# Depthwise convolution of 31 taps: TensorE's share goes from 14 taps on 64-wide diagonals to 16 taps on 32-wide diagonals, and the work around it moves between engines

## Chip, cores and metric

The kernel runs as one program on 1 core of a Trainium2 chip. The metric is the time of one execution in device microseconds (us); the median of several executions is given, and one further execution was profiled. A core has TensorE (PE, with its weight loads shown as PEld), VectorE (DVE), ScalarE (ACT), GpSimd (POOL) and SyncE (SP), each with its own instruction queue.

## What is computed

The reference is a two-layer mixed model over 512 tokens of width 1024 (an mLSTM layer, an attention layer, then a second block with its own two layers), all in float32. The change lies in one place, the convolution module of the second block's second layer:

```python
def conformer_conv(h, w_pw1, b_pw1, w_dw, b_dw, ln_g, ln_b, w_pw2, b_pw2):
    a, gate = jnp.split(h @ w_pw1 + b_pw1, 2, axis=-1)
    y = a * jax.nn.sigmoid(gate)
    y = lax.conv_general_dilated(y, w_dw[:, None, :], window_strides=(1,),
                                 padding=[(CONV_K // 2, CONV_K // 2)],
                                 dimension_numbers=('NWC', 'WIO', 'NWC'),
                                 feature_group_count=CONV_W) + b_dw
    y = jax.nn.silu(layernorm(y, ln_g, ln_b))
    return y @ w_pw2 + b_pw2
```

With `CONV_K = 31` and `CONV_W = 1024`, each channel is convolved along the 512 tokens with its own 31 taps.

## The kernel before

Activations lie with channels on the 128 partitions: a tile is 128 channels by 512 tokens, and a width of 1024 is 8 tiles. Every large product is done as three float32r products (hi by hi, lo by hi, hi by lo), so ScalarE makes a rounded copy of each weight chunk (`split_hi`, L509) and VectorE the remainder (`split_lo`, L514). A chunk is 128x1024; four slots are in flight, and SyncE loads the next chunk when VectorE has made the low part of the one before it in the slot.

The stage `p_1` computes `h @ w_pw1` in 8 groups. Group g gives one tile of `a` and one of `gate` in two PSUM banks of `G`: 48 matmuls of 128x128 by 512 (L2378), two chunks. Each engine goes through the groups in program order, and they meet through semaphores:

- ScalarE per group: two `split_hi` for the chunks of group g+2 (each waits until TensorE has used the chunk in that slot), then in `glu` the sigmoid of `gate` (L2094), and when VectorE has written `yp`, two copies of 64 partitions each into `yp_turned` (L2099), which holds the tile with its halves exchanged.
- VectorE per group: two `split_lo`, then in `glu` the product `yp` = (a + bias) * sigmoid (L2185), stored with 15 columns of zeros at both ends, and 17 taps of the convolution as shifted multiply-adds on `yp`, alternating between the accumulators `Y[g]` and `S[2]` (L2192, L2194 for taps 0 and 1, L2198 for taps 2 to 16). Then `total_low` (L2174) adds one PSUM bank of the group before, L2202 adds the two accumulators, `total_high` (L2180) adds the other bank.
- TensorE per group: the 48 matmuls, and behind them `taps(g-1)`, the other 14 taps of the group before: each tap is a product with a diagonal matrix, kept as 64x64 blocks in `tap_diag`. Seven taps read `yp` (L2015) and seven read `yp_turned` (L2018), so that the four 64x64 quarters of the array work on different data. Each of these float32 matmuls shows as two passes in the trace. Group g uses the banks 2p and 2p+1 of `M` (p = g mod 2), so `taps(g)` needs only that the totals of group g-2 are done (`cv_d >= g + 1`; two of the counts are there from the start).
- GpSimd makes the diagonals of a group in two operations of 128x448 (L2344, L2347) once the taps of two groups before are done.

After the last group VectorE adds the banks of group 7, TensorE sums the channels (L2027: 8 matmuls with `ones`, each waiting for its tile), VectorE subtracts the mean (L2212), ScalarE squares (L444), TensorE sums the squares (L2447), ten filling matmuls follow (`keep_warm`, L348), and then the stage `p_2`.

```python
                pe.wait_ge(cv_w, 2 * g + 2)
                wait_read(pe, "p_1", g)
                pe.wait_ge(cv_x, 2 * g + 4)
                pe.wait_ge(cv_d, g + 1)
```

## Time and profile before

| | |
|---|---|
| median of 3 runs | 2579.09 us (2578.74 to 2581.74) |
| the profiled execution, its own time | 2582.74 us |
| its span in the profile | 2580.9 us |
| PE busy | 2515.6 us, 97% of the span |
| DVE busy | 1544.0 us, 60% |
| ACT busy | 1028.7 us, 40% |
| POOL busy | 98.1 us, 4% |
| DMA | 266.86 MB, mean 103 GB/s |

The profile is of one execution. Its span runs from the first to the last instruction; the execution's own time is 1.8 us longer. Shares are averages over the whole program, in which the stage `p_1` takes some 150 us (from 2005 to about 2152 us), so what bounds that stage is read from its stretch of the trace. In timelines the first column is the start in us from the span's start, the second the duration, then engine, line, operation, output and inputs.

### The profile page before, as it was taken

How to read it: one execution, taken by the hardware profiler on the slowest of the kernel's cores; microseconds unless marked ns; L12 is line 12 of the kernel's file. 1: busy time of each engine (PE TensorE's matmuls, PEld its weight loads, DVE VectorE, ACT ScalarE, POOL GpSimd, SP SyncE). 2: the span in 40 equal slices, each digit the busy share in tenths (PEclk: the TensorE clock that was granted, in tenths of full speed). 3: DMA queues.
4: the chain of work that ended last, by engine and by line, in shares of the span. 5: the costliest groups of instructions: out<-in, count | busy, mean ns of one | idle time of the engine just before them, and what ended most of it. 6: DMA issues, size and time to landing. Idle time of an engine off the chain costs nothing.

```text
span 2580.9 us, 31514 instructions
## 1 busy us (share of the span) xinstructions
PE 2515.6 (97%) x12534; PEld 2005.1 (78%) x12534; DVE 1544.0 (60%) x2581; ACT 1028.7 (40%) x1583; POOL 98.1 (4%) x133
## 2 busy tenths in 40 slices
PE   7999999999999989999999998999999999999999
PEld 6887788888886667888878876888887665888887
DVE  6455775877455656746576256666654997533433
ACT  4444543434435555434345345423323324422323
POOL 0000001010000000000000000011100110000000
PEclk9999999999999999999999999999999999999999
DMA  5422335554221122332324221366642121233331
GB/s 155 134 83 90 92 96 171 154 175 137 67 82 58 55 69 76 96 98 83 100 88 153 82 66 42 124 195 194 189 146 90 58 66 45 86 98 98 98 95 52
DMA packets 285080, 266.86 MB, mean 103 GB/s; under 512 B 13331, under 2 KB 270663, under 8 KB 284935
## 3 DMA queue, kind: packets, MB, share of 16 engines
q1 hardware_dynamic: 268503, 210.33, 26.5%
q0 software_dynamic: 15024, 54.33, 7.1%
q8 instruction: 99, 1.62, 0.3%
q14 instruction: 46, 0.38, 0.0%
q10 hardware_dynamic: 1408, 0.20, 0.0%
HBM read 262.72 MB, written 2.10 MB: 103 GB/s over the span
## 4 chain that ended last, share of the span: by engine, by line
PE 87%; DVE 8%; ACT 2%; issue 2%; SPq 1%; DMA 0%; POOL 0%; ACTq 0%; DVEq 0%; POOLq 0%
PE G L2378 71%; PE G L2394 7%; DVE Y L2198 2%; DVE S L2198 1%; DVE w_lo L514 1%; PE M L2447 1%; PE M L818 1%; PE M L1196 1%; PE M L828 1%; PE M L1185 1%; PE M L1207 1%; PE M L1659 1%; PE M L1670 1%; PE M L2428 1%; DVE S L612 0%
## 5 line engine op out<-in xcount | busy, mean ns | idle before, releaser
L514 DVE TENSOR_TENSOR w_lo<-raw,w_hi 128x1024 fp32r<-128x1024 f32 x396 | 484.2, 1228 | 647.6 <-ACT w_hi L509 646.6
L2378 PE MATMUL G<-H_hi,w_hi 128*128 128x512 f32 (+1 forms) x2016 | 801.4, 398 | 4.9 <-DVE H_lo L377 1.6
L2378 PE MATMUL G<-H_hi,w_lo 128*128 128x512 f32 (+1 forms) x2016 | 783.9, 389 | 0.0
L2378 PE MATMUL G<-H_lo,w_hi 128*128 128x512 f32 (+1 forms) x2016 | 783.4, 389 | 0.0
L509 ACT ACTIVATE w_hi<-raw 128x1024 fp32r<-128x1024 f32 x396 | 416.9, 1056 | 890.2 <-PE G L2378 794.6
L2378 PEld LDWEIGHTS G<-H_hi,w_hi 128*128 128x128 f32 x2016 | 380.0, 188 | 108.9 <-issue 28.9
L2378 PEld LDWEIGHTS G<-H_hi,w_lo 128*128 128x128 f32 x2016 | 379.5, 188 | 79.3
L2378 PEld LDWEIGHTS G<-H_lo,w_hi 128*128 128x128 f32 x2016 | 379.9, 188 | 77.8 <-issue 3.8
L2378 PE MATMUL G<-hid_hi,w_hi 128*128 128x512 f32 x864 | 337.9, 391 | 5.3 <-DVE hid_lo L633 3.9
L2378 PE MATMUL G<-hid_lo,w_hi 128*128 128x512 f32 x864 | 336.9, 390 | 0.0
L2378 PE MATMUL G<-hid_hi,w_lo 128*128 128x512 f32 x864 | 336.7, 390 | 0.0
L2378 PEld LDWEIGHTS G<-hid_hi,w_hi 128*128 128x128 f32 x864 | 162.5, 188 | 42.0 <-DVE hid_lo L633 5.6
L2378 PEld LDWEIGHTS G<-hid_hi,w_lo 128*128 128x128 f32 x864 | 162.6, 188 | 33.9
L2378 PEld LDWEIGHTS G<-hid_lo,w_hi 128*128 128x128 f32 x864 | 162.6, 188 | 33.4
L2394 PE MATMUL G<-w_hi,H_hi 128*128 128x256 f32 x480 | 140.4, 292 | 3.5 <-DVE w_lo L514 2.1
L612 DVE SCALAR_TENSOR_TENSOR S<-SQ,VT,S 128x511 f32<-128x511 f32 (+1 forms) x176 | 128.2, 750 | 19.6 <-ACT S L574 16.5
L2394 PE MATMUL G<-w_hi,H_lo 128*128 128x256 f32 x480 | 136.5, 284 | 0.0
L2394 PE MATMUL G<-w_lo,H_hi 128*128 128x256 f32 x480 | 136.4, 284 | 0.0
L694 DVE SCALAR_TENSOR_TENSOR mod_acc<-mod_w,cs,mod_acc 128x512 f32<-128x512 f32 x168 | 125.9, 750 | 3.4
L672 POOL DMA_DIRECT2D mod_w<-in_w_mod x96 | 69.7, 726 | 1039.1 <-DVE mod_acc L694 470.6
L2394 PEld LDWEIGHTS G<-w_hi,H_hi 128*128 128x128 f32 x480 | 92.6, 193 | 14.9 <-issue 8.3
L574 ACT ACTIVATE S<-SQ,VT 128x512 f32<-128x512 f32 x88 | 67.0, 809 | 88.4 <-DVE SQ L619 88.4
(352 smaller groups left out, 2422.7 us busy)
## 6 DMA issues: line engine op xcount, KB each, us to landing
raw<-in_w_ff SPq DMA_DIRECT2D x128, 512.0 KB
mod_w<-in_w_mod POOLq DMA_DIRECT2D x96, 512.0 KB, 4.5
raw<-in_ffn_w_up SPq DMA_DIRECT2D x176, 256.0 KB
raw<-in_ffn_w_down SPq DMA_DIRECT2D x32, 512.0 KB
raw<-in_w_in SPq DMA_DIRECT2D x28, 512.0 KB
raw<-in_mlstm_w_in SPq DMA_DIRECT2D x24, 512.0 KB
raw<-in_kv_w SPq DMA_DIRECT2D x16, 512.0 KB
raw<-in_fox_w_qg SPq DMA_DIRECT2D x16, 512.0 KB
```

The costliest lines, as they stand in the source:

```text
L509: act.activation(w_hi[:, j, :], raw[:, j, :], ACT.Copy).then_inc(hi_done, 1)
L514: dve.tensor_tensor(w_lo[:, j, :], raw[:, j, :], w_hi[:, j, :], ALU.subtract).then_inc(lo_done, 1)
L574: act.activation(S[:, h, :], SQ[:, h, :], ACT.Identity, bias=VT[:, ds(t + cb, 1)], scale=VT[:, ds(t + (cw + 88), 1)]).then_inc(f_a, 1)
L612: return dve.scalar_tensor_tensor(S[:, h, k:T], SQ[:, h, 0:T - k], w, S[:, h, k:T], ALU.mult, ALU.add)
L672: pool.dma_start(mod_w[:, n % 2], src[:, 2 * quarter:2 * quarter + 2, block * 512:block * 512 + 512]).then_inc(mod_landed[n % 2], 16)
L694: one = dve.scalar_tensor_tensor(acc[:, cols], w, c, acc[:, cols], ALU.mult, ALU.add)
L818: return pe.matmul(M[:, bank, col:col + T - s * P], mK[hs, h // 2, s * P:s * P + P], mQ[hs, h // 2, s * P:T], start=(col == 0), stop=True, ...
L828: mm = pe.matmul(M[:, 2 + b // 2, (b % 2) * (P + 1):(b % 2 + 1) * (P + 1)], m_part(h, s)[:, (b - s) * P:(b - s) * P + P], mV[:, s, h, :], ...
L1185: mm = pe.matmul(fox_scores(n, e)[:, 0:(b + 1) * P], xQ[hs, q, b * P:b * P + P], xK[hs, q, 0:(b + 1) * P], start=True, stop=True)
L2198: link.post(dve.scalar_tensor_tensor(acc, yp[:, p:p + 1, j:j + T], tap(j), acc, ALU.mult, ALU.add))
L2378: mm = pe.matmul(G[:, 2 * p + m, 0:n], lw[:, k, ms], rh[:, t, 0:n], start=(t == 0 and q == 0), stop=(t == st["ktiles"] - 1 and q == 2), sk ...
L2394: mm = pe.matmul(G[:, 2 * p + b // 2, (b % 2) * GC:(b % 2) * GC + GC], lh[:, t, bs], rw[:, k, :], start=(t == 0 and q == 0 and b % 2 == 0) ...
```

## The change

TensorE gets 16 taps (15 to 30), and VectorE and ScalarE keep 15.

- A diagonal is now held as 32x32 blocks. `yp` and three turned copies `yp_turned[0..2]` (turned by 32, 64 and 96 partitions) feed four taps each. For each tap four matmuls of 32x32 by 512 run, one for each quarter r of the rows, writing quarter r+d of bank r. So all four banks of `M` hold one group, and the sum of the four is the 16 taps. `taps(g)` therefore waits for the totals of group g-1 (`cv_d >= g + 2`).
- ScalarE makes the first tap with the bias (`Y[g]`, new line L2115), starts four DMAs for the copies turned by 32 and 96, makes the copy turned by 64 itself as before, and makes the 16 diagonals of 128x32 of a group, ahead of that group's two `split_hi`. GpSimd's operations in this stage are gone.
- VectorE has 14 taps (1 to 14); `total` adds four banks instead of two.
- Six of the eight channel sums stand ahead of the last group's taps on TensorE.
- ScalarE makes the 32-wide identity and the turned tap columns (16 small operations) once, ahead of the stage `s0_up0`. VectorE's zero fill covers the edges of the four padded tiles only.

```diff
-PE_TAPS = 14
-HALF_TAPS = PE_TAPS // 2
+COPIES, COPY_TAPS = 4, 4
+PE_TAPS = COPIES * COPY_TAPS
 V_TAPS = CONV_K - PE_TAPS
+QP = P // COPIES
...
+            def channel_sum(t):
+                pe.wait_ge(cv_d, t + 3)
+                return pe.matmul(G[:, 0, :], ones[:], Y[:, t, :], start=(t == 0), stop=(t == 7), skip_group_check=True)
+
             def taps(g, p):
                 if g == 1:
                     pe.wait_ge(mod_ok, 4)
-                pe.wait_ge(cv_w, 2 * g + 2)
+                if g == DT - 1:
+                    wait_read(pe, "p_1", DT - 2)
+                    for t in range(DT - 2):
+                        channel_sum(t)
+                pe.wait_ge(cv_w, g + 1)
                 wait_read(pe, "p_1", g)
-                pe.wait_ge(cv_x, 2 * g + 4)
-                pe.wait_ge(cv_d, g + 1)
-                low, high = slice(0, HP), slice(HP, P)
-                for j in range(HALF_TAPS):
...
+                pe.wait_ge(cv_x, 2 * g + 2)
+                pe.wait_ge(cv_r[p], 64 * (g // 2 + 1))
+                pe.wait_ge(cv_d, g + 2)
+                for j in range(COPY_TAPS):
+                    for d in range(COPIES):
+                        source = yp_turned[d - 1] if d else yp
+                        tap = V_TAPS + COPY_TAPS * d + j
+                        for r in range(COPIES):
+                            rs, cs = quarter(r), quarter(r + d)
+                            mm = pe.matmul(M[cs, r, :], tap_diag[rs, p, COPY_TAPS * d + j, :], source[rs, p, tap:tap + T],
+                                           start=(j == 0), stop=(j == COPY_TAPS - 1), skip_group_check=True)
                 mm.then_inc(cv_pe, 1)
 
             linear("p_1", H_hi, H_lo, need=from_h("odd"), behind=taps)
...
+            channel_sum(DT - 2)
+            channel_sum(DT - 1).then_inc(cv_s, 1)
...
             held(act, "n_out", split_hi)
+            for r in range(COPIES):
+                act.activation(quarter_ident[quarter(r), :], ident[quarter(r), quarter(r)], ACT.Copy).then_inc(cv_h, 1)
+                for d in range(1, COPIES):
+                    first = ROW["w_dw_2"] + 8 * (V_TAPS + COPY_TAPS * d)
+                    act.activation(taps_turned[quarter(r), d - 1, :], VT[quarter(r + d), first:first + 8 * COPY_TAPS],
+                                   ACT.Copy).then_inc(cv_h, 1)
+            act.wait_ge(cv_h, 16)
             ffn2_act(act, 0, "odd")
...
                 wait_read(act, "p_1", g)
+                act.activation(Y[:, g, :], yp[:, p, 0:T], ACT.Identity, bias=vt("b_dw_2", g),
+                               scale=vt("w_dw_2", g)).then_inc(cv_i, 1)
+                for d, parts in ((1, ((0, 96, 32), (96, P, 0))), (3, ((32, P, 0), (0, 32, 96)))):
+                    for first, end, source in parts:
+                        act.dma_start(yp_turned[d - 1][first:end, p, PAD:PAD + T],
+                                      yp[source:source + end - first, p, PAD:PAD + T]).then_inc(cv_r[p], 16)
+                for to, hs in ((slice(HP, P), slice(0, HP)), (slice(0, HP), slice(HP, P))):
+                    act.activation(yp_turned[1][to, p, PAD:PAD + T], yp[hs, p, PAD:PAD + T], ACT.Copy).then_inc(cv_x, 1)
+
+            def diagonals(g, p):
                 act.wait_ge(cv_pe, g + 1)
...
+            steps = group_steps(act, "p_1", split_hi, glu)
+            for g in range(DT):
+                diagonals(g, g % 2)
+                for _ in range(3):
+                    next(steps)
...
+            def total(g, r):
+                if r:
+                    dve.wait_ge(cv_a, 3 * g + r)
+                else:
+                    dve.wait_ge(cv_pe, g + 3)
                 y = Y[:, g, :]
-                dve.tensor_tensor(y, y, M[:, 2 * p + 1, :], ALU.add).then_inc(cv_d, 1)
+                one = dve.tensor_tensor(y, y, M[:, r, :], ALU.add)
...
-                for j in range(2, V_TAPS):
+                link(dve.tensor_scalar(other, yp[:, p:p + 1, 1:1 + T], tap(1), None, ALU.mult))
+                link.post(dve.scalar_tensor_tensor(other, yp[:, p:p + 1, 3:3 + T], tap(3), other, ALU.mult, ALU.add))
+                dve.wait_ge(cv_i, g + 1)
+                for n, j in enumerate([2] + [j ^ 1 for j in range(4, V_TAPS - 1)] + [V_TAPS - 1]):
                     acc = other if j % 2 else y
-                    link.wait(1)
+                    if n:
+                        link.wait(0 if j == V_TAPS - 1 else 1)
                     link.post(dve.scalar_tensor_tensor(acc, yp[:, p:p + 1, j:j + T], tap(j), acc, ALU.mult, ALU.add))
                 link.wait(0)
                 if g:
-                    total_low(g - 1, 1 - p)
+                    total(g - 1, 0)
                 dve.tensor_tensor(y, y, other, ALU.add).then_inc(cv_v, 1)
                 if g:
-                    total_high(g - 1, 1 - p)
+                    for r in range(1, COPIES):
+                        total(g - 1, r)
```

How the instructions stand on two engines (in brackets the semaphores that a row waits for; rows that repeat are left out). VectorE, group 1 of `p_1` before: the first taps and the end of the group.

```order
L2185 SCALAR_TENSOR_TENSOR yp<-G,VT,S 128x512 [waits cv_pe,glu_a,chunk_used]
L2192 TENSOR_SCALAR Y<-yp,VT 128x512 [waits pair_read1]
L2194 TENSOR_SCALAR S<-yp,VT 128x512
L2198 SCALAR_TENSOR_TENSOR Y<-yp,VT,Y 128x512 [waits chain_d]
...
L2174 TENSOR_TENSOR Y<-Y,M 128x512 [waits cv_pe,chain_d]
L2202 TENSOR_TENSOR Y<-Y,S 128x512
L2180 TENSOR_TENSOR Y<-Y,M 128x512 [waits cv_a]
```

The same place of the changed kernel:

```order
L2221 SCALAR_TENSOR_TENSOR yp<-G,VT,S 128x512 [waits cv_pe,glu_a,chunk_used]
L2228 TENSOR_SCALAR S<-yp,VT 128x512 [waits pair_read1]
L2229 SCALAR_TENSOR_TENSOR S<-yp,VT,S 128x512 [waits chain_d]
L2235 SCALAR_TENSOR_TENSOR Y<-yp,VT,Y 128x512 [waits cv_i]
...
L2235 SCALAR_TENSOR_TENSOR Y<-yp,VT,Y 128x512 [waits chain_d] x2
L2212 TENSOR_TENSOR Y<-Y,M 128x512 [waits cv_pe,chain_d]
L2239 TENSOR_TENSOR Y<-Y,S 128x512
L2212 TENSOR_TENSOR Y<-Y,M 128x512 [waits cv_a] x3
```

Tap 0 has left VectorE, the first add into `Y` waits for ScalarE (`cv_i`), and four bank adds stand where two stood. ScalarE, from the last chunk held over from the stage before to the end of group 0, in the changed kernel (before, two small copies of 64x56 stood in the place of the 16 `tap_diag` rows, and nothing stood between the sigmoid and the copies of 64 partitions):

```order
L513 ACTIVATE w_hi<-raw 128x1024 [waits chunk_used,raw_landed3]
L2130 ACTIVATE tap_diag<-quarter_ident,VT 128x32 [waits cv_pe]
L2130 ACTIVATE tap_diag<-quarter_ident,VT 128x32 x3
L2130 ACTIVATE tap_diag<-quarter_ident,taps_turned 128x32 x12
L513 ACTIVATE w_hi<-raw 128x1024 [waits chunk_used,raw_landed0]
L513 ACTIVATE w_hi<-raw 128x1024 [waits chunk_used,raw_landed1]
L2112 ACT_TABLE_LOAD [waits pair_read0]
L2112 ACTIVATE S<-G,VT 128x512 [waits chunk_used]
L2115 ACTIVATE Y<-yp,VT 128x512 [waits pair_read0]
L2119 DMA yp_turned_150<-yp 96x512
...
L2122 ACTIVATE yp_turned_151<-yp 64x512 x2
```

TensorE at the last group, changed kernel; before, the last taps followed those of group 6 at once, and all eight channel sums (`G<-Y,ones`) came behind them:

```order
L2012 MATMUL G<-Y,ones 128x512 [waits cv_d,pair_read0]
L2012 MATMUL G<-Y,ones 128x512 [waits cv_d] x5
L2033 MATMUL M<-yp,tap_diag 32x512 [waits cv_r1,cv_x,cv_d,pair_read1,cv_w]
...
L2012 MATMUL G<-Y,ones 128x512 [waits cv_d] x2
L2468 MATMUL M<-SQ,ones 128x512 [waits n_sd,n_sq]
```

## Rows read from the trace of the kernel before

**Rows 1.** The page: busy time, share and instructions of each engine.

```profile
PE 2515.6 (97%) x12534; PEld 2005.1 (78%) x12534; DVE 1544.0 (60%) x2581; ACT 1028.7 (40%) x1583; POOL 98.1 (4%) x133
```

**Rows 2.** Timeline of DVE, group 1 (start us, us, engine, line, operation).

```profile
2035.97 0.74 DVE L2185 SCALAR_TENSOR_TENSOR yp<-G,VT,S 128x512 f32<-128x512 f32 x1
2036.75 0.55 DVE L2192 TENSOR_SCALAR Y<-yp,VT 128x512 f32<-128x512 f32 x1
2037.21 0.48 DVE L2194 TENSOR_SCALAR S<-yp,VT 128x512 f32<-128x512 f32 x1
2037.61 0.74 DVE L2198 SCALAR_TENSOR_TENSOR Y<-yp,VT,Y 128x512 f32<-128x512 f32 x1
...
2047.66 0.69 DVE L2174 TENSOR_TENSOR Y<-Y,M 128x512 f32<-128x512 f32 x1
2048.27 0.68 DVE L2202 TENSOR_TENSOR Y<-Y,S 128x512 f32<-128x512 f32 x1
...
2051.74 0.75 DVE L2185 SCALAR_TENSOR_TENSOR yp<-G,VT,S 128x512 f32<-128x512 f32 x1
```

**Rows 3.** Timeline of DVE, group 6 to the start of group 7.

```profile
2119.28 0.74 DVE L2185 SCALAR_TENSOR_TENSOR yp<-G,VT,S 128x512 f32<-128x512 f32 x1
...
2120.53 1.18 DVE L2194 TENSOR_SCALAR S<-yp,VT 128x512 f32<-128x512 f32 x1
2121.63 1.44 DVE L2198 SCALAR_TENSOR_TENSOR Y<-yp,VT,Y 128x512 f32<-128x512 f32 x1
...
2136.45 0.74 DVE L2185 SCALAR_TENSOR_TENSOR yp<-G,VT,S 128x512 f32<-128x512 f32 x1
```

**Rows 4.** Timeline of POOL, group 6.

```profile
2120.38 1.04 POOL L2344 TENSOR_TENSOR tap_diag<-half_ident,VT 128x448 f32<-128x448 f32 x1 [15.03 <-PE M L2018]
```

**Rows 5.** Timeline of PE: taps of group 0, first matmul after them, next taps.

```profile
2027.66 0.65 PE L2015 MATMUL M<-yp,tap_diag 64*64 64x512 f32 x2
...
2033.83 0.50 PE L2378 MATMUL G<-H_hi,w_hi 128*128 128x512 f32 x1
...
2044.94 0.65 PE L2015 MATMUL M<-yp,tap_diag 64*64 64x512 f32 x2
```

**Rows 6.** Timeline of ACT, then DVE, at the start of p_1.

```profile
2014.56 0.52 ACT L2103 ACTIVATE taps_turned<-VT 64x56 f32<-64x56 f32 x2
...
2016.95 1.06 ACT L509 ACTIVATE w_hi<-raw 128x1024 fp32r<-128x1024 f32 x1 [0.78 <-PE G L2378]
...
2019.33 0.69 ACT L2094 ACTIVATE S<-G,VT 128x512 f32<-128x512 f32 x1
...
2020.49 0.74 DVE L2185 SCALAR_TENSOR_TENSOR yp<-G,VT,S 128x512 f32<-128x512 f32 x1
```

**Rows 7.** Groups of instructions by shape, ACT (line engine op names shapes xcount | busy us, mean ns).

```profile
L1550 ACT ACTIVATE rm<-M 32x64 f32<-32x64 f32 x8 | 1.7, 213 | 0.2
```

**Rows 8.** Timeline of ACT (a DMA start), and the page's DMA issues (KB each, us to landing).

```profile
675.38 0.45 ACTq L2594 DMA_DIRECT2D gw_raw<-in_kv_w  x1
...
mod_w<-in_w_mod POOLq DMA_DIRECT2D x96, 512.0 KB, 4.5
```

**Rows 9.** Timeline of all engines, end of p_1.

```profile
2144.95 6.28 PE L2027 MATMUL G<-Y,ones 128*128 128x512 f32 x14
...
2149.95 0.68 DVE L2174 TENSOR_TENSOR Y<-Y,M 128x512 f32<-128x512 f32 x1
...
2150.67 0.69 DVE L2180 TENSOR_TENSOR Y<-Y,M 128x512 f32<-128x512 f32 x1
...
2152.57 1.89 DVE L2212 SCALAR_TENSOR_TENSOR Y<-G,Y 128x512 f32<-128x512 f32 x3 [1.22 <-PE G L2027]
```

**Rows 10.** Timeline of PE at 28 us, and the windows view (PEclk is granted clock).

```profile
28.40 0.62 PE L2453 MATMUL M<-H_hi,gw_hi 128*40 128x512 f32 x1 [3.30 <-DVE H_lo L465]
...
27.10:33.80 6.70, 5.40 (x13) 3.54 (x14) 6.70 (x11) 4.22 (x7) 0.00 (x0) 0.50 0.50 140
```

**Rows 11.** Timeline of PE at 1389 us: 64 passes of small matmuls.

```profile
1389.80 2.08 PE L1539 MATMUL M<-rm,sel 128*64 128x64 f32 x64
```

More of the change, by code:

```diff
@@ L249, in build @@
         yp = at("yp", 112 * K, [P, 2, T + 2 * PAD])
[L250 to L253 removed]
+        yp_turned = [at(f"yp_turned{d}", 117 * K + 4608 * (d - 1), [P, 2, T + 2 * PAD]) for d in range(1, COPIES)]
+        tap_diag = at("tap_diag", 131 * K, [P, 2, PE_TAPS, QP])
+        taps_turned = at("taps_turned", 169 * K, [P, COPIES - 1, 8 * COPY_TAPS])
+        quarter_ident = at("quarter_ident", 170 * K, [P, QP])
         G = ctx.enter_context(nc.psum_tensor("G", [P, 4, 512], F32))
@@ L319, in build @@
                              "fin_c").split()]
+        cv_i = sem("cv_i")
+        cv_r = [sem(f"cv_r{p}") for p in range(2)]
         TOKENS = [(hid_l, 1), (cv_pe, 2), (cv_d, 2)]
@@ L1964, in ffn2_dve, with quarter @@
                          ("odd", "final")[layer] if part == 3 else None)
+        def quarter(r):
+            return slice(QP * (r % COPIES), QP * (r % COPIES) + QP)
         def second_pe(pe, linear, linear_units, norm, from_h, squares_behind):
@@ L2021, in taps @@
                 mm.then_inc(cv_pe, 1)
             linear("p_1", H_hi, H_lo, need=from_h("odd"), behind=taps)
-            wait_read(pe, "p_1", DT - 2)
-            for t in range(DT):
-                pe.wait_ge(cv_d, t + 3)
-                mm = pe.matmul(G[:, 0, :], ones[:], Y[:, t, :], start=(t == 0), stop=(t == 7))
-            mm.then_inc(cv_s, 1)
+            channel_sum(DT - 2)
+            channel_sum(DT - 1).then_inc(cv_s, 1)
             norm("conf")
@@ L2161, in second_dve @@
             dve.wait_ge(chunk_used, used_after("s0_down3"))
-            dve.memset(yp_turned[:], 0.0)
-            link(dve.memset(yp[:], 0.0))
+            for tile in yp_turned + [yp]:
+                dve.memset(tile[:, :, 0:PAD], 0.0)
+                one = dve.memset(tile[:, :, PAD + T:], 0.0)
+            link(one)
             dve.wait_ge(mod_ok, 3)
@@ L2200, in glu @@
                 if g:
-                    total_low(g - 1, 1 - p)
+                    total(g - 1, 0)
                 dve.tensor_tensor(y, y, other, ALU.add).then_inc(cv_v, 1)
                 if g:
-                    total_high(g - 1, 1 - p)
+                    for r in range(1, COPIES):
+                        total(g - 1, r)
                 dve.wait_ge(cv_v, g + 1)
             groups(dve, "p_1", split_lo, glu)
-            total_low(DT - 1, 1)
-            total_high(DT - 1, 1)
+            for r in range(COPIES):
+                total(DT - 1, r)
             dve.wait_ge(cv_s, 1)
```

55 lines of the change are left out of this document (11 added, 44 removed).

## The prediction

> **What bounds the kernel now.** I read the page first, then the timeline of each engine over the stage p_1, then the waits there. TensorE is busy 97% of the span [rows 1], which suggests that taking TensorE time away is the prize. In this stage that is misleading: VectorE works without a pause from the first product yp at 2020.49 [rows 6] to the last bank add, which starts at 2150.67 and lasts 0.69, so to 2151.36 [rows 9]. No DVE row in between shows idle time. TensorE finished its last taps at about 2144.95, where the channel sums begin [rows 9], and then only followed VectorE. **VectorE's chain sets the end of the stage.** A group takes it 15.77 us where nothing disturbs it (2035.97 to 2051.74) [rows 2], but 17.17 in group 6 (2119.28 to 2136.45) [rows 3]. The difference is two operations that are 0.7 us too long (1.18 against 0.48, 1.44 against 0.74 [rows 2, 3]), and they run just while GpSimd makes diagonals [rows 4]. Added over the stage, ten VectorE operations between 2020 and 2152 are longer than their kind by 6.6 us. TensorE needs 6.17 for the taps (2027.66 to 2033.83) and 11.11 for the 48 matmuls with the changeover (to 2044.94), 17.28 a group [rows 5]; so it is nearly as full.
>
> **The change, part by part.**
> (a) *GpSimd's diagonals go.* The stretched operations return to their usual length: -6.6 us. If that stretching had another cause, this gain is zero, its other end.
> (b) *VectorE's operations.* Per group go one TENSOR_SCALAR, 0.46 apart, and two multiply-adds of 0.67 (15 of them in 2037.61 to 2047.66) [rows 2]: 1.79, times 8 is -14.3. Two more bank adds stand at 0.61 each (2047.66 to 2048.27) [rows 2]; 14 of them lie before the end of group 7: +8.5. Where an operation needs the one just before it, it starts 0.72 instead of 0.61 after it (2149.95 to 2150.67 [rows 9]), 0.12 more; new places are behind tap 1, ahead of tap 14, and in the third and fourth bank add, 30 in all: +3.6. Net -2.2. The undisturbed period becomes 15.77 - 1.79 + 1.22 + 0.48 = 15.7. ScalarE's first tap takes about the 0.69 of the sigmoid row [rows 6] and VectorE reaches the add that waits for it 1.2 after yp, so that wait costs nothing, as long as ScalarE stands waiting for yp.
> (c) *Start of the stage.* 16 diagonals now stand ahead of the first two hi splits. The nearest ScalarE row is 0.213 for 32x64 [rows 7]; with the scale operand I take 0.23, 3.7 in all (3.4 to 4.4). Before, the second split began at 2016.95 after a wait of 0.78 [rows 6]; now it begins at 2014.56 + 3.7 + 1.0 = 2019.2, which is 2.2 later, and the sigmoid ends at 2020.02 + 2.2 = 2022.2. yp moves from 2020.49 to 2022.3: +1.8.
> (d) *Diagonals, DMAs and copies inside the stage.* ScalarE per group: splits 2.1, sigmoid 0.7, tap 0.7, four DMA starts at 0.45 [rows 8] 1.8, two copies 1.3, diagonals 3.7: 10.3 of 15.7, and from yp to the next group's first split 7.5 us, while the chunk that this split waits for comes free some 6 us after yp. Cover is thus about 5 us before VectorE asks. The DMAs carry 512 KB; the nearest row lands 512 KB 4.5 us after its issue [rows 8], and the taps start 12.6 us after yp. Zero, unless they take twice as long as that.
> (e) *The taps on TensorE.* 64 matmuls in two passes are 128 passes. Before, 56 passes, four side by side, made 14 rounds in 6.17, 0.43 to 0.44 each [rows 5]. If 16 run side by side it is 8 rounds, 3.5, and I take T = 3.7 for the stagger of 16 starts. The trace shows only four abreast; with four it would be 32 rounds, 13.8. The start of passes doesn't forbid sixteen: 64 passes of 128x64 start within 1.86 us, 29 ns apart [rows 11], and 16 times 29 ns is 0.46, about a round. I take the near end for that reason. The Trainium skill ("TensorE: Matmul & The Clock Gate", Part 3: Packing small matmuls) gives a measured speedup of 10.6, not 16, for sixteen 32x32 tiles at 512 columns; by that figure T would be an estimated 5.2 and the total some 7 us above my forecast. No row here has more than four tiles.
> (f) *The new wait.* taps(g) waits for the bank adds of group g-1, the last thing VectorE does in group g. Behind it on TensorE's queue are the 48 matmuls of group g+2. From the end of VectorE's group: T, 11.1 for these, 1.06 for the second hi split [rows 6], about 0.2 for the signals; VectorE wants that split 1.2 after its next group ends. So the wait is free while T + 12.4 is below 15.7 + 1.2, **T below 4.5**. Beyond that each microsecond of T costs one in each of 7 groups.
> (g) *The end.* Group 7's adds now begin only when its own taps are done, and these begin only when VectorE's group 7 ends: 2149.95 [rows 9] + 1.8 - 6.6 - 2.2 = 2142.9. Ahead of that, TensorE did the taps of group 6 (from 2127.2) and six channel sums, 12 passes of 0.43 [rows 9], and then stands idle from about 2136.3, 6.6 us. After an idle 3.30 us the trace has the clock at half: 27.1 to 33.8 was granted 0.50, 5.4 us of it after work resumed at 28.40 [rows 10]. So I expect the last taps at 1.2 GHz at first: eight rounds of 0.87 are 7.0 if it lasts; if it ends after 5.4 as there, six rounds are slow and two are not, 6.1. Their ends are 3.7 (no fall) and 7.0; I take 6.5. Then four dependent adds, 0.72 each, 2.9. End: 2142.9 + 0.2 + 6.5 + 2.9 = 2152.5 against 2151.36: **+1.1 us**. What follows (L2212 at 1.2 after the last add [rows 9]) stays if the clock is back by then.
> (h) *One-time set-up.* 16 small operations, 3.7 us, ahead of ScalarE's first split of s0_up0. The slot they delay is wanted by TensorE two groups (some 20 us) later, so zero; without that cover 3.7. The shorter zero fill lies beside ScalarE's norm: zero.
>
> Sum: (c) +1.8, (a) -6.6, (b) -2.2, (g) 0.2 + 6.5 + 2.9 less the 1.4 that the last two adds took before, +8.2: +1.2, with rounding +1.1. On the profiled execution (2582.74, of which the span is 2580.9) that is 2583.8; on the median of 2579.09, from which that execution stands 3.6 up, **2580.2**.
>
> **Rivals.**
> *A: the clock doesn't fall, or costs nothing.* T = 3.7 in (g) too: 2.8 us less, 2577.4. For: in 2141 to 2152 TensorE often waited and kept its clock. Against: the idle stretch now is twice the one of [rows 10]. 12%.
> *B, on the other side: the array doesn't keep 16 tiles abreast.* With eight abreast T is 16 rounds, 7.0. It decides from T = 4.5 on: (7.0 - 4.5) * 7 = 17.5, and the last taps take 3 to 4 more, 2601. For: nothing in the trace has run sixteen. Against: [rows 11]. 12%.
> *B2: the rounds of sixteen are stretched,* each pass being held up by the loads and starts of its neighbours, as if eleven ran abreast: 12 rounds of 0.44, T = 5.3, (5.3 - 4.5) * 7 = 5.6, and 1.8 more at the last taps, 2587.6. For: in [rows 11] sixteen starts already take 0.46, more than the 0.43 of a round, before any stream is shared. Against: the four of [rows 5] show no such loss. 12%. The skill's speedup of 10.6 for sixteen tiles lies in this case.
> *C: the half clock lasts.* If it falls again in the pauses around the last adds, the channel sum and 16 passes of squares, 0.43 each, run at half for a while: +2 to +4 on top, 2582 to 2584. 15%.
> *D: ScalarE or the DMAs are late* (diagonals at 0.3 instead of 0.23, DMA starts of 1 us): +3 to +8. 6%.
> *E: VectorE gains more*, for instance the dependent starts cost nothing: -3.6, 2576.6, and with A 2573.8. 8%.
>
> **How the numbers follow.** The forecast itself has 35%. Under 0.2% (5.2 us) a measurement of this kernel can't tell a difference, so the forecast, A, C, half of D and 3 of E's 8 are "same", 68%. Slower by more is B, B2 and the other half of D, 27%; faster by more needs E together with A, 5%. The range reaches down to 2576 (A, or E alone) and up to 2591 (B2 with its bounds), and leaves out B and the far part of E, 17%.
>
> **What the changed profile would show.** No GpSimd operation in the stage; VectorE periods of 15.7 without a 1.2 or 1.4 us tap; yp of group 0 at about 2022.3; taps of 3.7 us from first to last pass, right behind VectorE's last bank add; TensorE idle about 1 us a group and 6.6 before the last taps, with 0.5 clock in them; the last bank add's end near 2152.5. Taps longer than 4.5, VectorE waiting for w_hi or the sigmoid in the middle of the stage, or GpSimd's absence leaving the long taps as they were, would make it wrong.

## The result, and the profile after

The changed kernel takes 2586.14 us (median of 20 runs, 2581.31 to 2589.84) against 2580.02 for the kernel before in the same comparison (20 runs, 2578.74 to 2585.8): ratio 1.0021, 95% interval 1.0015 to 1.0028. It is **slower by about 6 us**. The forecast was +1.1; the time lies inside its range, 2576 to 2591, on its slow side. The profiled execution took 2589.17 us with a span of 2587.3, 6.4 above that of before.

The page, busy time of each engine:

```profile
PE 2507.9 (97%) x13110; PEld 2008.5 (78%) x13110; DVE 1532.0 (59%) x2579; ACT 1065.0 (41%) x1733; POOL 77.5 (3%) x116
```

Against [rows 1] VectorE is busy 12 us less, TensorE 8 us less, and the span is longer. The windows view of the whole stage (from the first matmul of `p_1` to the first of `p_2`; columns: window, its length, busy us of PE, PEld, DVE, ACT and POOL, granted clock, DMA share, GB/s), of before and then of after:

```profile
2005.68:2167.10 161.42, 157.45 (x884) 97.19 (x885) 155.60 (x222) 50.49 (x67) 20.04 (x16) 1.00 0.19 56
```

```profile
2005.43:2173.54 168.11, 150.83 (x1460) 100.56 (x1461) 145.69 (x214) 83.51 (x201) 0.00 (x0) 0.94 0.28 79
```

VectorE's work fell by 9.9 us, TensorE's by 6.6 although its clock was 0.94 instead of 1.00, and the stage grew by 6.7. From `p_2` to the end both kernels take the same 413.8 us, so all of the difference is in here. Below, "from the start" counts from the first matmul of `p_1` (2005.68 before, 2005.43 after).

Timeline of DVE of the changed kernel, one undisturbed group and the start of the next:

```profile
2084.69 0.75 DVE L2221 SCALAR_TENSOR_TENSOR yp<-G,VT,S 128x512 f32<-128x512 f32 x1
2085.47 0.49 DVE L2228 TENSOR_SCALAR S<-yp,VT 128x512 f32<-128x512 f32 x1
2085.99 0.75 DVE L2229 SCALAR_TENSOR_TENSOR S<-yp,VT,S 128x512 f32<-128x512 f32 x1
...
2095.46 0.68 DVE L2239 TENSOR_TENSOR Y<-Y,S 128x512 f32<-128x512 f32 x1
2096.06 2.12 DVE L2212 TENSOR_TENSOR Y<-Y,M 128x512 f32<-128x512 f32 x3
...
2100.54 0.75 DVE L2221 SCALAR_TENSOR_TENSOR yp<-G,VT,S 128x512 f32<-128x512 f32 x1
```

The period is 15.85 here and 15.69 to 15.85 in four of the groups (where [rows 2] had 15.77 and [rows 3] 17.17), and no tap is stretched. This part came out as forecast. What did not is seen on TensorE. Its timeline, the taps of groups 0, 1 and 7 and the end:

```profile
2028.55 0.63 PE L2033 MATMUL M<-yp,tap_diag 32*32 32x512 f32 x4 [1.07 <-DMA yp_turned<-yp]
...
2032.94 0.50 PE L2399 MATMUL G<-H_hi,w_hi 128*128 128x512 f32 x1
...
2048.49 1.08 PE L2033 MATMUL M<-yp,tap_diag 32*32 32x512 f32 x4 [4.38 <-DVE Y L2212]
...
2134.27 5.42 PE L2012 MATMUL G<-Y,ones 128*128 128x512 f32 x12
2146.00 1.08 PE L2033 MATMUL M<-yp,tap_diag 32*32 32x512 f32 x4 [6.32 <-DVE Y L2212]
...
2155.21 1.13 PE L2012 MATMUL G<-Y,ones 128*128 128x512 f32 x2 [1.96 <-DVE Y L2212]
2157.78 10.34 PE L2468 MATMUL M<-SQ,ones 128*128 128x512 f32 x16 [1.45 <-ACT SQ L448]
```

and the windows in which the clock was at half:

```profile
2047.45:2054.25 6.80, 5.76 (x99) 2.71 (x102) 6.69 (x10) 1.17 (x2) 0.00 (x0) 0.50 0.43 123
2143.00:2149.80 6.80, 3.80 (x66) 1.61 (x68) 2.78 (x5) 0.00 (x0) 0.00 (x0) 0.50 0.01 2
2156.70:2163.50 6.80, 5.72 (x7) 2.42 (x8) 6.80 (x14) 2.62 (x5) 0.00 (x0) 0.50 0.01 2
```

**Three falls of TensorE's clock to 1.2 GHz** stand where the stage of before has none. One begins in the 4.38 us that TensorE waits in front of the taps of group 1, one in the 6.32 in front of the last taps, one in the pauses around the last sums. The last taps were forecast slow; the third fall is rival C; the first stands in no case of the prediction. What that one does to VectorE, from its timeline one group later:

```profile
2063.94 1.22 DVE L518 TENSOR_TENSOR w_lo<-raw,w_hi 128x1024 fp32r<-128x1024 f32 x1
2067.86 1.23 DVE L518 TENSOR_TENSOR w_lo<-raw,w_hi 128x1024 fp32r<-128x1024 f32 x1 [2.70 <-ACT w_hi L513]
2069.00 0.75 DVE L2221 SCALAR_TENSOR_TENSOR yp<-G,VT,S 128x512 f32<-128x512 f32 x1
```

ScalarE's split waits for a chunk that TensorE gives back late, and VectorE loses 2.70: that group takes 18.46 us (from yp at 2050.54 to 2069.00). And the end of the stage on DVE (the mean subtraction, L2250, is L2212 in [rows 9]):

```profile
2143.73 2.12 DVE L2212 TENSOR_TENSOR Y<-Y,M 128x512 f32<-128x512 f32 x3
2152.30 2.85 DVE L2212 TENSOR_TENSOR Y<-Y,M 128x512 f32<-128x512 f32 x4 [6.45 <-PE M L2033]
2156.37 4.28 DVE L2250 SCALAR_TENSOR_TENSOR Y<-G,Y 128x512 f32<-128x512 f32 x7 [1.22 <-PE G L2012]
```

### The profile page after: what moved, and what is told of

The parts are those of the page before. It is cut to its first block, busy times and chain, and to the rows that moved or that the text cites. A ratio compares the mean times of both kernels' runs of the same rounds, so it can differ in the third digit from the quotient of the medians.

```text
span 2587.3 us, 32819 instructions
## 1 busy us (share of the span) xinstructions
PE 2507.9 (97%) x13110; PEld 2008.5 (78%) x13110; DVE 1532.0 (59%) x2579; ACT 1065.0 (41%) x1733; POOL 77.5 (3%) x116
## 3 DMA queue, kind: packets, MB, share of 16 engines
q10 hardware_dynamic: 3968, 4.39, 0.6%
## 4 chain that ended last, share of the span: by engine, by line
PE 88%; DVE 6%; ACT 3%; issue 2%; SPq 1%; DMA 0%; POOL 0%; ACTq 0%; DVEq 0%; POOLq 0%
PE G L2399 72%; PE G L2415 6%; PE M L2468 1%; DVE Y L2235 1%; PE M L2033 1%; PE M L822 1%; PE M L1200 1%; PE M L832 1%; ACT w_hi L513 1%; PE M L1189 1%; DVE S L2235 1%; PE M L1211 1%; PE M L1663 1%; DVE w_lo L518 1%; PE M L1674 1%
## 5 line engine op out<-in xcount | busy, mean ns | idle before, releaser
L2415 PE MATMUL G<-w_hi,H_hi 128*128 128x256 f32 x480 | 140.4, 293 | 3.5 <-DVE w_lo L518 2.1
```

Of the source, the lines that this page charges most:

```text
L2415: mm = pe.matmul(G[:, 2 * p + b // 2, (b % 2) * GC:(b % 2) * GC + GC], lh[:, t, bs], rw[:, k, :], start=(t == 0 and q == 0 and b % 2 == 0) ...
```

## The experiments

A *fall* is a stretch in which the granted clock is at half; a *filler* is a multiply whose result nothing reads. Theory 1: the loss is the clock's falls, the one in group 1 and the one in the squares. The rivals: the falls only fill time in which TensorE would wait anyway, so that taking them away gives little; or the new taps themselves (T), beyond their threshold, hold the stage. All times are medians with their own comparison; "stage" is from the first matmul of `p_1` to the first of `p_2` in the profiled execution (before 161.4, after 168.1).

| run | us | ratio to before, 95% | stage |
|---|---|---|---|
| fill17 | 2580.84 | 1.0002 (0.9993 to 1.0011) | 162.1 |
| fill1 | 2583.89 | 1.0015 (1.0006 to 1.0024) | 165.2 |
| pool_busy | 2591.93 | 1.0048 (1.0036 to 1.0061) | 173.0 |
| mid | 2580.36 | 1.0001 (0.9993 to 1.0010) | 161.3 |
| mid_behind | 2576.75 | 0.9987 (0.9978 to 0.9996) | 158.4 |
| early | 2576.99 | 0.9986 (0.9977 to 0.9994) | 157.5 |
| early_fill | 2576.55 | 0.9985 (0.9976 to 0.9995) | 157.8 |
| sums_back | 2587.68 | 1.0029 (1.0019 to 1.0038) | 168.4 |
| best_order | 2576.77 | 0.9982 (0.9973 to 0.9991) | 158.2 |
| before_act_diag | 2580.31 | 0.9996 (0.9987 to 1.0005) | 161.5 |
| long_taps | 2592.56 | 1.0046 (1.0032 to 1.0059) | 172.4 |
| best_cover | 2572.71 | 0.9969 (0.9959 to 0.9979) | 153.7 |

### Fill the waits with multiplies that nothing reads

```diff
+            def filler(p, count):
+                for _ in range(count):
+                    pe.matmul(G[:, 2 * p, 0:GC], ident[:], VT[:, 0:GC], start=True, stop=True, skip_group_check=True)
...
                 pe.wait_ge(cv_r[p], 64 * (g // 2 + 1))
+                filler(p, {1: 8, 7: 16}.get(g, 0))
                 pe.wait_ge(cv_d, g + 2)
...
             channel_sum(DT - 2)
+            filler(1, 5)
             channel_sum(DT - 1).then_inc(cv_s, 1)
+            filler(1, 4)
```

**fill17**, all of it. Expected: 

> The changed kernel with filling matmuls (256 columns, into a free bank of G) where TensorE waits: 8 ahead of the taps of group 1, 16 ahead of those of group 7, 5 and 4 around the last channel sum. Theory 1 (half clock): the changed kernel loses 2.7 us behind group 1 and 2.3 us in the last taps and 2.6 us in the squares to stretches at 1.2 GHz; with the filler the granted clock stays at 1.0 from 1962 to the end, taps of groups 1 and 7 take 3.9 like the others, and the median falls from 2586 to 2579 (2577.5 to 2580.5), with less spread from run to run. Theory 2 (the new order of waits alone costs the time, the clock is a by-product): the median stays within 1.5 us of 2586.

Measured 2580.84. The windows view of its stage:

```profile
2003.05:2165.20 162.15, 157.91 (x1526) 110.50 (x1527) 145.81 (x214) 83.56 (x201) 0.00 (x0) 1.00 0.30 82
```

The clock is 1.00, TensorE does *more* work than in the changed kernel, and the stage is 6.0 us shorter. The falls are gone and only fillers were added, so the falls cost 5 to 6 us. Timelines of PE and DVE at its last taps:

```profile
2142.01 0.63 PE L2038 MATMUL M<-yp,tap_diag 32*32 32x512 f32 x4
...
2146.58 2.85 DVE L2219 TENSOR_TENSOR Y<-Y,M 128x512 f32<-128x512 f32 x4 [5.71 <-PE M L2038]
```

From the first of the last taps to the first bank add it is 4.57 us, where the changed kernel has 6.30 (2146.00 to 2152.30): the fall there cost 1.7. The time of fill17 is that of the kernel before, so without any fall the change is worth about nothing. Some 1 us of the time is the fillers' own: those in front of the last taps (7.1 us of them) end after VectorE's group, and the taps begin 1.1 after it instead of 0.15. That adds up: 2.9 (fill1, below), 1.7 and 2.6 for the squares (7.60 us here, 10.34 in the changed kernel) are 7.2, less the fillers' 1.0 is 6.2, beside the 6.0 measured.

**fill1**, the eight in front of the taps of group 1 alone (`{1: 8}`, nothing else). Expected: 

> The changed kernel with 8 filling matmuls ahead of the taps of group 1 only. Theory 1 (half clock): only the fall at about 42 us into the stage goes, the taps of group 1 take 3.9 and VectorE's third period 15.7 instead of 18.5; 2.8 us less than the changed kernel, about 2583.4. Theory 2 (that period is long for another reason): unchanged at 2586.

Measured 2583.89, stage 2.9 shorter. Timeline of PE:

```profile
2041.68 3.61 PE L2012 MATMUL G<-VT,ident 128*128 128x256 f32 x16
...
2046.39 0.63 PE L2038 MATMUL M<-yp,tap_diag 32*32 32x512 f32 x4 [1.10 <-DVE Y L2217]
```

The fall in group 1 is gone and the group that took 18.46 takes 15.77; the two later falls stay. So this fall belongs to this pause, and it is 2.9 of the 6. The pause as such costs nothing here: the fillers fill most of it, the taps still begin only when VectorE has ended its bank adds, and the time goes down.

### Move the bank adds inside VectorE's group

```diff
                     link.post(dve.scalar_tensor_tensor(acc, yp[:, p:p + 1, j:j + T], tap(j), acc, ALU.mult, ALU.add))
+                    if g and 5 <= n < 5 + COPIES:
+                        total(g - 1, n - 5)
                 link.wait(0)
-                if g:
-                    total(g - 1, 0)
                 dve.tensor_tensor(y, y, other, ALU.add).then_inc(cv_v, 1)
-                if g:
-                    for r in range(1, COPIES):
-                        total(g - 1, r)
```

**mid**, this alone: the banks come free while VectorE still multiplies. Expected: 

> The changed kernel with the four bank adds of group g-1 in the middle of VectorE's chain of group g instead of at its end. Theory (the wait of taps(g) for the end of VectorE's group g, with the clock falls it brings, is what the change pays): taps(g) no longer wait, TensorE runs ahead, the last taps are over before VectorE ends its group 7, two dependent starts a group go as well; the last bank add ends at about 2144 instead of 2155, median 2574 (2572 to 2577). Rival (the adds wait for the taps in the middle of the chain, or TensorE becomes the bound): VectorE shows waits on the banks and the median stays above 2580.

**mid_behind**, and ScalarE's diagonals behind its group instead of ahead of it. Expected: 

> As the run with the bank adds in the middle, and ScalarE makes the diagonals of group g behind its part of group g instead of ahead of its splits. Theory (the 16 diagonals of group 0 ahead of the first splits delay the first yp by 1.2 to 1.8 us): yp of group 0 at 2020.2 to 2020.5 instead of 2021.7, median 1.2 to 1.8 below the run with the adds in the middle alone, about 2573. Rival (TensorE sets the pace by then, or the first taps come too late): the same time as that run, or up to 3 us above.

Mid measured 2580.36 and missed by 6 us; mid_behind 2576.75, a miss by 4. In both the taps of group 1 wait 1.6 us at most and the clock stays, VectorE's period is 15.56, and the first `yp` of mid_behind is 1.8 us earlier, as expected of the diagonals. What was missed is the end. Timeline of PE of mid:

```profile
2125.02 5.42 PE L2012 MATMUL G<-Y,ones 128*128 128x512 f32 x12
2136.20 1.07 PE L2033 MATMUL M<-yp,tap_diag 32*32 32x512 f32 x4 [5.76 <-DVE Y L2212]
```

The adds of group 6 are not early enough for the last taps: 5.76 us of waiting, a fall, slow taps, and a second fall in the squares (16 passes in 10.49 us). Mid_behind has the same wait and the same two falls. Interleaving one add per tap holds the banks until the fourth is through.

**early**: the adds behind the first taps (n from 1), diagonals behind, and all the sums back behind the last taps. Expected: 

> Bank adds of group g-1 directly behind the first taps of VectorE's group g (2.6 us after yp instead of 5.9), diagonals behind ScalarE's part of the group, and all eight channel sums behind the last taps as in the kernel before. Theory (TensorE's idle stretch ahead of the last taps ends with the adds, and the sums then fill the next one): the last taps run while VectorE is still in group 7, at full clock in 3.9; from the first matmul of p_1 to the first of p_2 it is 153 to 156 us (158.4 with the adds in the middle, 161.4 in the kernel before), median 2572 to 2575. Rival (VectorE now reaches the adds before TensorE has done the taps and waits each group): periods of 16 and more, no better than 2577.

**early_fill**: the same with three fillers behind the last sum. Expected: 

> As the run with early adds, with 3 filling matmuls behind the last channel sum. Theory 1 (a fall of the clock in the pause there costs 2.6 us in the 16 passes of squares): 0 to 2.6 us below the run with early adds alone, and less spread. Theory 2 (the clock holds there anyway once the sums stand in front): the same time within 1 us.

2576.99 and 2576.55: the same as mid_behind and no better. Timelines of PE, ACT and DVE of early:

```profile
2128.53 2.64 ACT L2128 ACTIVATE tap_diag<-quarter_ident,taps_turned 128x32 f32<-128x32 f32 x12
...
2130.12 0.68 DVE L2210 TENSOR_TENSOR Y<-Y,M 128x512 f32<-128x512 f32 x1
...
2131.22 1.08 PE L2029 MATMUL M<-yp,tap_diag 32*32 32x512 f32 x4 [8.82 <-ACT tap_diag L2128]
...
2137.91 7.13 PE L2012 MATMUL G<-Y,ones 128*128 128x512 f32 x16
```

The last diagonals, queued behind ScalarE's sigmoid, tap and copies, came last, at 2131.17: 8.82 us of waiting and a fall of 10.2. But the banks weren't free in time either. The last bank add ends at 2130.80, only 0.4 earlier, so diagonals on time would have gained no more than that. The mean then waits for sixteen passes of sums. The fillers changed nothing, because here the squares ran at full clock without them.

**sums_back**: the changed kernel with its six early sums moved back behind the last taps, nothing else. Expected: 

> The changed kernel with one part undone: all eight channel sums stand behind the last taps, as before. TensorE is idle for 12 instead of 7 us ahead of the last taps, so that fall stays, and 5.1 us of sums move behind them, where TensorE else waits for the adds. [...] Theory 2 (the six sums ahead are worth their 5.1 us on the path): median 2589 to 2591.

```diff
-                if g == DT - 1:
-                    wait_read(pe, "p_1", DT - 2)
-                    for t in range(DT - 2):
-                        channel_sum(t)
...
-            channel_sum(DT - 2)
+            wait_read(pe, "p_1", DT - 2)
+            for t in range(DT - 1):
+                channel_sum(t)
```

Measured 2587.68, which is 1.5 above the changed kernel and below theory 2's 2589. Timelines of DVE and PE at its end:

```profile
2157.58 4.88 DVE L2248 SCALAR_TENSOR_TENSOR Y<-G,Y 128x512 f32<-128x512 f32 x8 [4.14 <-PE G L2012]
...
2158.99 7.71 PE L2466 MATMUL M<-SQ,ones 128*128 128x512 f32 x16 [1.45 <-ACT SQ L448]
```

With TensorE at work through the adds there is no third fall, and the squares take 7.71 instead of 10.34, 2.6 less; but the mean begins 4.14 instead of 1.22 after the last add, 2.9 more. A pause removed by work that is on the path gives back what it gains.

### GpSimd, TensorE's bound and the size of T

**pool_busy**: the changed kernel, and on GpSimd the two operations of 128x448 a group that it had before, on data nobody reads.

```diff
+            for t in range(DT):
+                pool.wait_ge(cv_pe, t + 1)
+                for half in range(2):
+                    pool.wait_ge(cv_h, 16 + max(0, 2 * t + half - 1))
+                    pool.tensor_tensor(spare_out[:, half], spare_in, spare_in, ALU.mult).then_inc(cv_h, 1)
```

Expected: 

> The changed kernel with two GpSimd products of 128x448 per group into memory that nobody reads, started when the kernel before started its diagonals. Theory (VectorE's stretched operations come from GpSimd working at the same time): two VectorE operations per group are 0.7 longer again, the undisturbed period of 15.7 becomes 17.1, the median rises by 7 to 10 us to 2593 to 2596. Rival (the stretch had another cause, such as the diagonals' reads of the taps): no stretched operation, the median within 2 us of 2586.

Measured 2591.93, some 6 above the changed kernel and 1 below what was expected: the last four periods are 17.04, but those of groups 1 and 2 are no longer than they were (15.68 and 18.15). Timelines of POOL and DVE:

```profile
2103.86 2.36 POOL L2379 TENSOR_TENSOR spare_out<-ident 128x448 f32<-128x448 f32 x2 [14.69 <-PE M L2033]
...
2104.00 1.43 DVE L2235 SCALAR_TENSOR_TENSOR S<-yp,VT,S 128x512 f32<-128x512 f32 x1
2105.35 1.42 DVE L2235 SCALAR_TENSOR_TENSOR Y<-yp,VT,Y 128x512 f32<-128x512 f32 x1
```

Two multiply-adds of 0.75 become 1.43 and 1.42, just beside GpSimd, which does not touch their data. So the stretching in [rows 3, 4] was GpSimd's, whatever it computes; by which way the one holds up the other these runs don't show.

**before_act_diag**: the kernel *before*, its fourteen diagonals made by ScalarE behind its group.

```diff
-                pe.wait_ge(cv_w, 2 * g + 2)
+                pe.wait_ge(cv_w, g + 1)
...
+            def diagonals(g, p):
+                act.wait_ge(cv_pe, g + 1)
+                for j in range(PE_TAPS):
+                    col = ROW["w_dw_2"] + 8 * (V_TAPS + j) + g
+                    w = (VT[:, col:col + 1] if j < HALF_TAPS else
+                         taps_turned[:, 8 * (j - HALF_TAPS) + g:8 * (j - HALF_TAPS) + g + 1])
+                    one = act.activation(tap_diag[:, p, j, :], half_ident[:], ACT.Copy, scale=w)
+                one.then_inc(cv_w, 1)
```

Expected: 

> The kernel before with one thing changed: its fourteen diagonals a group are made by ScalarE behind its own group instead of by GpSimd, which is idle in the stage. VectorE keeps its seventeen taps. Theory: VectorE's multiplies lose the 6.6 us that GpSimd's writes cost them in all, but the kernel before has 28 passes of 128 columns for the taps of a group, and TensorE's group (17.2 us in rows of before) is then nearer to the bound than VectorE's 15.8, so of the 6.6 us only part shows: 2577 to 2578 us. Rival: TensorE was waiting for VectorE and not the other way round; all of the 6.6 shows, 2573.5 us.

Measured 2580.31, ratio 0.9996: not even the 3 us of the theory. Timelines of DVE in group 5 and of PE and DVE at the end:

```profile
2095.82 1.23 DVE L514 TENSOR_TENSOR w_lo<-raw,w_hi 128x1024 fp32r<-128x1024 f32 x1 [1.16 <-ACT w_hi L509]
2096.96 0.75 DVE L2204 SCALAR_TENSOR_TENSOR yp<-G,VT,S 128x512 f32<-128x512 f32 x1
...
2137.12 0.65 PE L2015 MATMUL M<-yp,tap_diag 64*64 64x512 f32 x2 [1.78 <-ACT tap_diag L2116]
...
2150.47 4.88 DVE L2231 SCALAR_TENSOR_TENSOR Y<-G,Y 128x512 f32<-128x512 f32 x8 [4.05 <-PE G L2027]
```

VectorE's periods are 15.77 three times and then 17.03, 17.27 and 17.28: TensorE's 17.28 [rows 5] is reached, and VectorE waits for split weights. (TensorE's taps are 56 passes of 512 columns a group, not the 28 of 128 that the expectation names.) The last add ends 2.75 us earlier, which is the theory's 2 to 3; the last taps then wait for ScalarE's diagonals and the sums come after them, so the mean begins 4.05 after the last add and 0.1 us later than before. So of GpSimd's 6.6 us the old taps let through 2.75, because behind them TensorE's group is the longer one, and the order at the end took those. Whether another order at the end would have kept the 2.75 was not tried.

**long_taps**: the changed kernel with one tap step of each copy issued twice (it accumulates that step's products twice, so its output is another one).

```diff
-                for j in range(COPY_TAPS):
+                for j in (0, 1, 1, 2, 3):
```

Expected: 

> The changed kernel with one of the four tap steps of every copy issued twice on TensorE, so 20 passes of 16 tiles instead of 16 a group (the products of one tap of each copy are accumulated twice, so the output differs). From the first tap to TensorE's next wide multiply 4.4 us become about 5.4. The prediction said that T is free below 4.5 us. If the threshold holds, TensorE's slack of a third of a us a group is used up and the rest shows in each of seven groups, about 0.7 us each: 2591 to 2592 us, and the clock's falls in group 1 and in the last group may go or shrink. Rival: the slack between the engines is larger than the small idle rows say, 2587.5 us or less.

Measured 2592.56. From the first tap to the next wide matmul the changed kernel needs 4.39 us (2028.55 to 2032.94), this one 1.05 more, 5.44. Timelines of DVE and PE:

```profile
2082.70 0.75 DVE L2221 SCALAR_TENSOR_TENSOR yp<-G,VT,S 128x512 f32<-128x512 f32 x1
...
2099.25 0.75 DVE L2221 SCALAR_TENSOR_TENSOR yp<-G,VT,S 128x512 f32<-128x512 f32 x1
...
2080.29 0.63 PE L2033 MATMUL M<-yp,tap_diag 32*32 32x512 f32 x4
...
2096.85 0.63 PE L2033 MATMUL M<-yp,tap_diag 32*32 32x512 f32 x4
```

A period of 16.55, 0.86 above the 15.69 of an undisturbed group. If each microsecond above the threshold costs one, the threshold is 5.44 - 0.86 = 4.6: the prediction's 4.5, and the changed kernel stands 0.2 below it. The way to it is another, though. The taps here show no wait for the banks (the bank adds are over at 2079.63, 0.66 before the taps at 2080.29), and 16.55 is TensorE's own group, 5.44 + 11.11. So what holds the stage beyond the threshold is TensorE's own work, and the threshold is the T at which that equals VectorE's group, 15.69 - 11.11 = 4.58.

### Put together

**best_order**. The changed kernel with the adds of group g-1 behind VectorE's first taps (all four at once in group 7), diagonals behind ScalarE's group, but those of group 7 ahead of its splits, the six early sums kept, and fillers: three ahead of the last taps, ten ahead of the last sum and three behind it (256 columns each, not the 128 that the expectation names).

```diff
             for g in range(DT):
-                diagonals(g, g % 2)
                 for _ in range(3):
                     next(steps)
+                if g < DT - 1:
+                    diagonals(g, g % 2)
+                if g == DT - 2:
+                    diagonals(DT - 1, 1)
...
+                    if g == DT - 1 and n == 1:
+                        for r in range(COPIES):
+                            total(g - 1, r)
+                    if 0 < g < DT - 1 and 1 <= n < 1 + COPIES:
+                        total(g - 1, n - 1)
```

Expected: 

> The changed kernel with the four adds of group g-1 right behind the first taps of VectorE's group g (all four at once in group 7), ScalarE's diagonals behind its own group, except group 7's, which stand ahead of its splits; the six sums stay ahead of the last adds; three extra 128-column multiplies of TensorE ahead of the last group's taps, ten ahead of the last of the six sums and three behind it, all into banks that nothing reads. What the earlier runs lacked together: last adds end near 137.3 us from the first multiply of p_1 (early had 138.8 with the clock's fall in the last taps, 8.8 us of which TensorE waited for diagonals), squares at the full clock behind a gap of 1.2 us instead of 4.1, p_2's first multiply near 153 us (early 157.5). Expected 2572 us, 2570 to 2575. The other view, that TensorE's own work holds the stage by now and early's 2577 is the floor: 2576 or more.

Measured 2576.77, a miss by 4.8. Timeline of PE:

```profile
2120.52 5.42 PE L2016 MATMUL G<-Y,ones 128*128 128x512 f32 x12
2128.78 2.90 PE L2012 MATMUL G<-VT,ident 128*128 128x256 f32 x6 [2.85 <-DMA yp_turned<-yp]
2131.61 1.08 PE L2038 MATMUL M<-yp,tap_diag 32*32 32x512 f32 x4
```

With adds and diagonals out of the way the transfer of the copies is last. The fillers stood behind the wait for it: TensorE paused 2.85 us, the clock fell, and the three fillers (six passes) took 2.90 instead of the 1.46 that the same three take behind the last sum, on the path. Cover has to stand *ahead* of the wait that comes last.

**best_cover**. Expected: 

> best_order with its extra multiplies moved. There the three stood behind the wait for the copies' transfer, so TensorE was idle for 2.85 us before them, the clock fell at 127.9, and the three ran at half of it: the last taps began 2.8 us after the transfer had landed and took 5.4. Now six stand ahead of that wait, right behind the six sums, and nine instead of ten ahead of the last sum. Expected: no fall of the clock in the stage, last taps at 128.6 from the first multiply of p_1 and 3.9 us long, last adds end 137.4 (VectorE's own end, no wait for taps), squares from 140.1, p_2 at 153.2 (best_order 158.2), so 2572 us, 2570.5 to 2574. The other view, that those 5 us of TensorE's chain are hidden behind VectorE or come back later: 2576 or more.

```diff
                     for t in range(DT - 2):
                         channel_sum(t)
+                    filler(0.5, 6)
...
-                filler(p, {7: 3}.get(g, 0))
...
-            filler(1, 10)
+            filler(1, 9)
```

(the first argument now picks a bank of `G` that is free). Measured 2572.71 us, 0.9969 of before (0.9959 to 0.9979), 7.8 us faster than before, where the changed kernel is 6.1 slower. Its stage and its last taps:

```profile
2003.45:2157.10 153.65, 151.06 (x1496) 104.40 (x1497) 144.94 (x214) 83.34 (x201) 0.00 (x0) 1.00 0.32 87
```

```profile
2128.80 2.75 PE L2012 MATMUL G<-VT,ident 128*128 128x256 f32 x12
...
2132.29 0.63 PE L2038 MATMUL M<-yp,tap_diag 32*32 32x512 f32 x4 [0.74 <-DMA yp_turned<-yp]
...
2138.03 2.85 DVE L2222 TENSOR_TENSOR Y<-Y,M 128x512 f32<-128x512 f32 x4
```

VectorE does the work of the changed kernel, no less; TensorE is busy 98% of the stage at full clock. VectorE's groups take 15.56 without a wait, and TensorE's taps start 15.50 apart, its own 4.39 + 11.11: the two engines are level, and neither holds up the other in the steady groups.

## Why the prediction came out as it did

Counted from the start of the stage (2005.68 before, 2005.43 after). One more line of the timeline of DVE of before, the last bank add of group 1, which ends at 2049.55 and is used in (f):

```profile
2048.87 0.68 DVE L2180 TENSOR_TENSOR Y<-Y,M 128x512 f32<-128x512 f32 x1
```

- **(a) GpSimd's share, (b) VectorE's operations: right.** 15.7 forecast, 15.69 measured, no stretched operation, and pool_busy brings the stretching back at will. The end of VectorE's group 7 was forecast at 2142.9 - 2005.68 = 137.2; the changed kernel has it at 140.4, of which 2.9 is the fall in group 1. Without that fall it is 137.5, and fill1 has 137.7.
- **(c) The start: right in kind.** yp(0) moves from 14.8 to 16.2, +1.4 against +1.8. Sixteen diagonals took 3.4 us, 0.21 each, the value of [rows 7] itself; the addition for the scale operand was not needed.
- **(d) DMAs and copies: right.** The copies' transfer held up only the taps of group 0, by 1.07, where TensorE had time (it waited 4.38 in the next group anyway). The four DMA starts took 2.56 us instead of 1.8, which cost nothing here. That the transfer would be the last wait once the others are gone was seen only in best_order.
- **(e) T: mis-sized, and no matter.** 4.39 instead of 3.7. One pass at a time, at 0.43, 128 passes would take 55.0; 55.0 / 4.39 is 12.5 abreast, between the forecast's sixteen and B2's eleven. The Trainium skill ("TensorE: Matmul & The Clock Gate", Part 3: Packing small matmuls) has 10.6, from which an estimate of 5.2 came; the trace disagrees, with its 12.5 over eight rounds of sixteen in a row. With 5.2 each group would cost 0.6 more (by the threshold of 4.6 that long_taps gives). B is out, and B2 did not decide.
- **(f) The threshold: right in size; "TensorE idle about 1 us a group": the step that failed.** The threshold is 4.6 against 4.5, though by TensorE's own group and not by the loop through the bank adds that the sum followed (long_taps). But the waits of a group were averaged over the stage. In steady groups TensorE waits 0.5 us or less for the banks; in group 1 it waits 4.38. It is through with its wide matmuls at 2044.1 (2048.49 less 4.38), because VectorE's group 0 has no bank adds and TensorE began it early, while the banks come free only at the end of VectorE's group 1. This was in reach: yp(0) at 2022.3, a first group of 13.3 (15.7 less four adds of 0.61), and 13.5 from yp(1) to the end of the bank adds (15.7 less the 2.2 from the end of the last add, 2049.55, to 2051.74 in [rows 2]) give 2049.1; TensorE, from its first taps at 2027.66 [rows 5], or 1.8 later, would be ready 3.7 + 11.1 after them, at 2042.5 to 2044.3. The 5 to 6.6 us between are longer than the 3.30 after which [rows 10] has the clock at half. The prediction applied that row to the end of the stage and not to its beginning: +2.9 us.
- **(g) The end: right, in part by luck.** From the end of VectorE's group 7 to the last add's end 9.3 us against 9.6 forecast (0.2 + 6.5 + 2.9), an idle of 6.3 against 6.6, taps from first to last pass of 5.6. Inside the 6.5 two errors cancel: at full clock it is 4.57 from the first of these taps to the first add (fill17) where 3.7 was taken, and the fall adds 1.7 where 2.8 was.
- **"What follows stays if the clock is back by then": it was not.** The third fall makes the way from the mean subtraction to `p_2` 17.2 instead of 14.5, +2.6. That is rival C, with the size it named (+2 to +4); sums_back and fill17 show it as the fall's. Its 15% was too little beside 35% for a forecast with exactly one fall: the pauses of 1.96 and 1.45 around the last adds followed in a few microseconds on one of 6.3.
- **(h) Set-up:** no difference is seen ahead of the stage.

Sum: +1.1 forecast, +2.9 for group 1, +2.6 for C, -0.3 for (g), and 0.3 for VectorE's end, gives +6.6; the stage has +6.7 and the medians +6.1. The direction was forecast, but not the size: +6.1 lies beyond the 5.2 us that the prediction set as the least clear difference, which it gave 27% to the slower side. And it came from two falls of one kind, not from the sixteen tiles that most of the slower chance had been laid on. That the range reached this far is luck: the forecast and C end at 2584, and beyond that it rests on B2 and D, neither of which happened. Had all the falls been avoided, the change would have been worth about nothing (fill17). With the bank adds earlier, the diagonals behind and the two later falls left in it is worth 3.7 us (mid_behind), with every pause short or covered 7.8 (best_cover).

## What to carry to other kernels

A new wait in a periodic pipeline has to be timed in its first and last turn by themselves: the engines do not start the pipeline in step, and a wait of half a microsecond or less in steady groups was 4.4 us in the first that had it. Such a pause of TensorE can cost time even where the wait itself costs none, by the work at 1.2 GHz after it (fill1: 2.9 us); look for what holds the wait (here the four banks, released only at the end of a group) before filling it, and if it is filled, put the filler ahead of the wait that comes last. When one late resource is removed, look up the next in line: banks, diagonals and transfer were each last in turn here, some of them by less than half a microsecond, and only the version that moved the first two and covered the wait for the third got the whole gain.

## What the runs showed of the hardware

- Sixteen 32x32 tiles by 512 columns in two passes are sustained at 12.5 abreast (4.39 us for 128 passes), better than had been feared and worse than sixteen.
- GpSimd stretches VectorE operations with which it shares no data: beside two GpSimd operations of 1.2 us, two multiply-adds take 0.68 us more each (0.75 to 1.43), and the group 1.35 (17.04 against 15.69).
- The cost of a fall isn't read from its length. The same 6.8 us at half clock cost 2.9 in group 1, where TensorE had no slack behind it, and 1.7 in the last taps (5.61 us from first to last pass against 3.87). In the pauses of 1.45 in front of the squares the clock stayed where TensorE had just run without a gap (sums_back), and fell where 1.96 of waiting stood a little ahead of it.
- Executions of one program differ in granted clock too: the 20 of the changed kernel lie between 2581.31 us at a mean clock of 0.993 and 2589.84 at 0.987, so one execution alone does not show a difference of 3 us.
